# Values of block 2's attention made token-major, in eight weight units ahead of the head pairs

## The reference

```python
def dilated_attention_mixer(u, w_in, w_out, cos, sin):          # layer 0
    q, k, v = jnp.split(u @ w_in, 3, axis=-1)
    q = apply_partial_rope(split_heads(q, A_HEADS), cos, sin)   # 16 heads of 64
    k = apply_partial_rope(split_heads(k, A_HEADS), cos, sin)
    v = split_heads(v, A_HEADS)
    ...  # three banded softmaxes, combined by their denominators
    return merge_heads(o).astype(u.dtype) @ w_out

def differential_attention_mixer(u, w_in, w_out, ..., sub_g, cos, sin, layer_idx):  # layer 1
    q, k, v = jnp.split(u @ w_in, 3, axis=-1)
    ...  # 8 heads, each with two q/k halves of 64 and a value of 128
        sc = jnp.einsum('bhcqd,bhckd->bhcqk', qblk, k) * scale
        p = jax.nn.softmax(sc, axis=-1)
        a = p[:, :, 0] - lam * p[:, :, 1]
        return jnp.einsum('bhqk,bhkd->bhqd', a, v)
    o = rms_norm(o, sub_g) * (1.0 - lam_init)
    return merge_heads(o).astype(u.dtype) @ w_out
```

## Time and profile before

| | |
|---|---|
| median of three runs | 3102.79 us (3102.61, 3102.79, 3104.38) |
| span of the profiled execution | 3103.3 us |
| its time less its span | no separate time of it is shown; the span lies 0.5 us over the median and inside the three runs |
| TensorE busy | 3044.2 us, 98% |
| VectorE busy | 1775.0 us, 57% |
| ScalarE busy | 1269.9 us, 41% |
| GpSimd busy | 302.2 us, 10% |
| granted TensorE clock, mean | 0.996 |
| chain that ended last: TensorE | 83% of the span |
| the same chain: VectorE | 7% |

### The profile page before, as it was taken

The page is one execution under the profiler, slowest core; times in us unless marked ns, Lnnn a source line. Parts: engine busy times, 40 slices in busy tenths (PEclk is TensorE's granted clock), DMA queues, the critical chain, the costliest instruction groups (busy, mean ns, idle before and its releaser), DMA issues.

```text
span 3103.3 us, 38484 instructions
## 1 busy us (share of the span) xinstructions
PE 3044.2 (98%) x15248; PEld 2423.5 (78%) x15248; DVE 1775.0 (57%) x2564; ACT 1269.9 (41%) x2084; POOL 302.2 (10%) x257
## 2 busy tenths in 40 slices
PE   7999999999999999999999999999999999999998
PEld 6777888887777888887667878888866688788886
DVE  7765543457765544457775635344577755354444
ACT  6654422245654322344444534232344444342322
POOL 2011100011011100012001102000110011020001
PEclk9999999999999999999999999999999999999999
DMA  3111333232111223322112322332211123123332
GB/s 139 55 49 55 95 97 100 95 95 82 56 46 65 95 95 98 98 95 74 55 55 89 122 68 82 95 99 99 89 61 55 48 95 111 66 89 97 101 95 82
DMA packets 73726, 259.14 MB, mean 84 GB/s; under 512 B 8020, under 2 KB 10200, under 8 KB 73176
## 3 DMA queue, kind: packets, MB, share of 16 engines
q1 hardware_dynamic: 72824, 252.99, 25.8%
q0 software_dynamic: 736, 3.87, 0.4%
HBM read 254.73 MB, written 2.10 MB: 83 GB/s over the span
## 4 chain that ended last, share of the span: by engine, by line
PE 83%; DVE 7%; issue 6%; ACT 1%; DVEq 1%; POOLq 1%; DMA 1%; POOL 0%; ACTq 0%; SPq 0%
PE bank L563 68%; PE bank L493 2%; PE bank L1125 1%; DVE w_lo L2177 1%; PE bank L1136 1%; PE bank L779 1%; PE bank L1350 1%; PE bank L1329 1%; POOLq L3057 1%; PE bank L1080 1%; PE bank L1146 1%; PE bank L1150 1%; PE bank L809 0%; PE bank L822 0%; DMA w_raw<-weights 0%
## 5 line engine op out<-in xcount | busy, mean ns | idle before, releaser
L563 PE MATMUL bank<-a_hi,w_hi 128*128 128x512 f32 x2120 | 848.5, 400 | 18.8 <-DVE w_lo L2177 15.2
L563 PE MATMUL bank<-a_hi,w_lo 128*128 128x512 f32 x2120 | 828.4, 391 | 0.0
L563 PE MATMUL bank<-a_lo,w_hi 128*128 128x512 f32 x2120 | 827.5, 390 | 0.0
L2177 DVE TENSOR_TENSOR w_lo<-w_raw,w_hi 128x1024 fp32r<-128x1024 f32 (+1 forms) x474 | 609.4, 1287 | 285.7 <-ACT w_hi L1456 284.1
L1456 ACT ACTIVATE w_hi<-w_raw 128x1024 fp32r<-128x1024 f32 (+1 forms) x474 | 495.5, 1046 | 417.7 <-DMA w_raw<-weights 417.5
L563 PE MATMUL bank<-b_hi,w_hi 128*128 128x512 f32 (+1 forms) x1516 | 572.0, 377 | 2.6 <-DVE w_lo L2177 1.5
L563 PE MATMUL bank<-b_hi,w_lo 128*128 128x512 f32 (+1 forms) x1516 | 563.7, 372 | 0.0
L563 PE MATMUL bank<-b_lo,w_hi 128*128 128x512 f32 (+1 forms) x1516 | 563.5, 372 | 0.0
L563 PEld LDWEIGHTS bank<-a_hi,w_hi 128*128 128x128 f32 x2120 | 399.4, 188 | 120.1 <-issue 22.2
L563 PEld LDWEIGHTS bank<-a_hi,w_lo 128*128 128x128 f32 x2120 | 399.2, 188 | 85.7
L563 PEld LDWEIGHTS bank<-a_lo,w_hi 128*128 128x128 f32 x2120 | 399.8, 189 | 83.1 <-issue 3.8
(11 more groups left out here) (339 smaller groups left out, 3216.6 us busy)
## 6 DMA issues: line engine op xcount, KB each, us to landing
w_raw<-weights SPq DMA_DIRECT2D x458, 512.0 KB, 3.5
w_raw<-weights SPq DMA_DIRECT2D x16, 384.0 KB, 3.0
x<-x SPq DMA_DIRECT2D x8, 256.0 KB, 7.2
mem<-mem POOLq DMA_DIRECT2D x2, 1024.0 KB, 5.1
out<-x SPq DMA_DIRECT2D x8, 256.0 KB, 2.1
mem<-mem SPq DMA_DIRECT2D x1, 1024.0 KB, 11.7
ple<-ple POOLq DMA_DIRECT2D x2, 512.0 KB, 3.9
o<-c_level SPq DMA_DIRECT2D x1, 512.0 KB
```

The costliest lines, as they stand in the source:

```text
L563: last = mm(bank[unit_bank(u) if at is None else at][:, 0:cols], w[:, u % SLOTS, ks], t[:, k, 0:cols], start=(k == begun and n == 0), stop ...
L2177: tt(w_lo[:, u % SLOTS, w], w_raw[:, u % SLOTS, w], f32(w_hi[:, u % SLOTS, w]), ALU.subtract).then_inc(w_lo_ready, 1)
```

## The change

The stream of units gets another order: q and k of pair 0, then all values, then q and k of pairs 1 to 7. The values come in eight transfers that hold two contraction tiles of four units each. TensorE multiplies them the other way round (`values`): the activations of 128 tokens stand still and 512 value features stream, so that the result is token-major at once, in four banks for each half of the features. ScalarE copies each bank to `v` with the norm's root as its scale. Transposes, evictions and copies of the value units in the pairs are gone, and so is one unit in each pair. The half units stand in four places of a pair instead of six, and turn 3 of a pair moves ahead of the first score of the next. In layer 0 the last pair multiplies three output units at once, and five units follow; its output tiles stand one by one between the steps. All `kept_busy` of the two mixers go, but for five matmuls in layer 1. ScalarE's and VectorE's lists are rewritten to fit.

```diff
+order += [(at, 8, 0), (at + 8, 8, 0)]
+order += [(at + 16 + 4 * side, 0, rows) for side in range(2) for rows in range(4)]
+order += [(at + 8 * part + r, 8, 0) for r in range(1, 8) for part in range(2)]
...
+V_BANKS = (((3, 4, 6, 5), (2, 4, 6, 5)), ((3, 4, 6, 2), (5, 4, 6, 2)))
...
-        pe.wait_ge(bank_free, first if u == first + 2 else u - 1)
+        pe.wait_ge(bank_free, u - 1)
+        last.then_inc(unit_done, 1)
+        c.unit += 1
+def values(side, midway=None):
+    for j in range(4):
+        u = c.unit
+        pe.wait_ge(w_lo_ready, u + 1)
+        if side == 0 and j == 0:
+            pe.wait_ge(bank_free, first)
+        for tb in range(ST):
+            if side == 1 and j == 0:
+                pe.wait_ge(bank_free, first + 2 + tb)
+            out_ = bank[V_BANKS[l][side][tb]][:, :].rearrange("p (n c) -> p n c", n=4)
+            for i in range(2):
+                k = 2 * j + i
+                whole, rest = (t[:, u % SLOTS, :].rearrange("p (n c) -> p n c", n=4)[:, :, qs(i)] for t in (w_hi, w_lo))
+                for n, (x_, w_) in enumerate(((a[0], whole), (a[0], rest), (a[1], whole))):
+                    last = mm(out_, x_[:, k, qs(tb)], w_, start=(k == 0 and n == 0), stop=(k == 7 and n == 2))
+            if midway is not None and j == 0 and tb == 1:
+                midway()
         last.then_inc(unit_done, 1)
         c.unit += 1
...
         if p == 0:
-            pe.wait_ge(bank_free, first + 3)
+            pe.wait_ge(bank_free, first + 2 + V_UNITS)
...
-half(1)
-for r in range(1, PAIRS + 1):
-    more = r < PAIRS
-    if more:
-        half(0)
...
+    values(0, midway=columns_and_spread)
+values(1)
+half(0)
+for r in range(1, PAIRS):
+    half(1)
+    if r > 1:
+        turn(r - 2, 3)
     score(r - 1, 0)
-    if r >= 2:
+    half(0)
+    if r > 1:
         outputs(r - 2)
-    if more:
-        half(1)
     score(r - 1, 1)
     turn(r - 1, 0)
-    if more:
+    half(1)
+    score(r - 1, 2)
+    turn(r - 1, 1)
+    if r < PAIRS - 1:
         half(0)
     score(r - 1, 3)
     turn(r - 1, 2)
-    values(r - 1)
...
+    if diff and r > 1:
         tile_sums(r - 2)
+p = PAIRS - 1
+turn(p - 1, 3)
+score(p, 0)
+outputs(p - 1)
...
-    out_begun((4, 5))
-    outputs(PAIRS - 1)
-    kept_busy(F_S[0], 3, 2 * P)
-    out_begun((6, 7))
-a_units(6)
+    three = (0, 1, 2)
+    out_begun(0, three)
+    score(p, 1)
+    turn(p, 0)
+    out_begun(1, three)
+    score(p, 2)
+    turn(p, 1)
+    out_begun(2, three)
+    score(p, 3)
+    turn(p, 2)
+    out_begun(3, three)
+    turn(p, 3)
+    out_begun(4, three)
+    outputs(p)
+    out_begun(5, three)
+    out_begun(6, three)
+    out_begun(7, three)
+    a_units(5)
...
+def values(side):
+    act.wait_ge(unit_done, first + 6 + 4 * side)
+    for tb in (1, 2, 3, 0):
+        f(v[:, tb, 4 * P * side:4 * P * (side + 1)], bank[V_BANKS[l][side][tb]][:, :], ACT.Copy,
+          scale=root_cols[:, tb:tb + 1]).then_inc(bank_free, 1)
...
+ahead(first + 8)
+act.wait_ge(bank_free, first + 2)
+values(0)
+ahead(first + 12)
+values(1)
+for r in range(1, PAIRS):
+    if r > 1:
+        copies(r - 2, 3)
     exps(r - 1, 0)
+    ahead(first + 2 * r + 10)
     exps(r - 1, 1)
     copies(r - 1, 0)
+    if diff and r > 1:
         norm_square(r - 2)
     exps(r - 1, 2)
     copies(r - 1, 1)
+    ahead(first + 2 * r + 11)
     exps(r - 1, 3)
     copies(r - 1, 2)
...
+p = PAIRS - 1
+ahead(first + 26)
 if diff:
+    norm_root(0, 0, 24)
+copies(p - 1, 3)
+if not diff:
+    out_rounded((0,))
+exps(p, 0)
+if not diff:
+    out_rounded((1,))
+exps(p, 1)
+copies(p, 0)
+exps(p, 2)
+copies(p, 1)
+out_rounded((1,) if diff else (2, 3))
+exps(p, 3)
+copies(p, 2)
+out_rounded((2, 3) if diff else (4, 5))
+copies(p, 3)
...
+dve.wait_ge(bank_free, first + 2 + V_UNITS)
+for r in range(1, PAIRS):
+    if r > 1:
+        normalise(r - 2, 3)
     maxima(r - 1, 0)
+    evict(r, 0)
     normalise(r - 1, 0)
+    rope_sin(r, 0)
+    ahead(first + 2 * r + 10)
+    if r > 1:
         take(r - 2)
     maxima(r - 1, 1)
+    rope_add(r, 0)
     normalise(r - 1, 1)
+    if diff and r > 1:
         dve.drain()
         norm_clamped(r - 2)
+    evict(r, 1)
     maxima(r - 1, 2)
+    rope_sin(r, 1)
     normalise(r - 1, 2)
     maxima(r - 1, 3)
+    rope_add(r, 1)
+    ahead(first + 2 * r + 11)
+p = PAIRS - 1
+normalise(p - 1, 3)
+ahead(first + 26)
+maxima(p, 0)
...
+normalise(p, 0)
+take(p - 1)
...
+else:
+    out_low((1,))
+normalise(p, 1)
+maxima(p, 2)
...
+    out_low((1,))
+else:
+    out_low((2,))
+normalise(p, 2)
+maxima(p, 3)
...
```

More of the change, by code:

```diff
@@ L1152, in outputs, with out_begun @@
                     last.then_inc(f_out, 1)
[L1154 to L1170, removed]
+                def out_begun(k, begun=(0, 1)):
+                    u = c.unit
+                    if k == 0:
+                        pe.wait_ge(w_lo_ready, u + begun[-1] + 1)
+                        pe.wait_ge(bank_free, first + 3 * PAIRS)
+                        if 2 in begun:
+                            pe.wait_ge(f_sin, 2 * (pairs + PAIRS))
+                    pe.wait_ge(h_ready, c.since(h_ready, k + 1))
+                    for v_ in begun:
+                        last = products(u + v_, k, a, 8, S, at=(W_BANK + (OUT_THIRD,))[v_])
                         if k == 7:
                             last.then_inc(unit_done, 1)
[L1173 to L1176, removed]
+                    if k == 7:
+                        c.unit += len(begun)
+                        c.add(h_ready, 8)
                 def norm_sums(tiles):
                     pe.wait_ge(n_squared, tiles[-1] + 1)
+                    pe.wait_ge(n_applied, 6)
                     for i, p in enumerate(tiles):
@@ L1226, in fused @@
                         half(0)
-                    else:
-                        kept_busy(W_BANK[0] if diff else F_R, 3, 2 * P)
-                    score(r - 1, 2)
-                    if not more and diff:
-                        norm_spread(0)
-                        norm_spread(1)
-                    turn(r - 1, 1)
-                    if more:
-                        half(1)
-                    else:
-                        kept_busy(F_R, 3, 2 * P)
-                    score(r - 1, 3)
@@ L2737, in out2, with kept @@
                 for k in range(8 if mixed else 6):
-                    step(lambda u, b: dve.tensor_copy(y[:, k, :], b[:, :]).then_inc(bank_free, 1))
+                    def kept(u, b):
+                        b = bank[OUT_THIRD] if mixed and l == 0 and k == 2 else b
+                        dve.tensor_copy(y[:, k, :], b[:, :]).then_inc(bank_free, 1)
+                    step(kept)
                     if mixed and k == 2:
@@ L2842, in fused @@
                 rope_sin(0, 0)
-                evict(0, 2)
+                ahead(first + 4)
                 rope_add(0, 0)
                 rope_sin(0, 1)
-                ahead(first + 4)
+                ahead(first + 5)
                 rope_add(0, 1)
-                for r in range(1, PAIRS + 1):
-                    more = r < PAIRS
-                    if more:
-                        ahead(first + 3 * r + 2)
-                    if l == 0 and r == 1:
-                        dve.wait_ge(dil_landed, c.count(dil_landed, 16))
+                c.unit += V_UNITS
```

211 lines of the change are left out of this document (92 added, 119 removed).

## The result

The changed kernel takes 3140.07 us (median of four runs, 3138.57 to 3141.63), the kernel before 3103.43 beside it. The ratio is 1.0116 with a 95% interval of 1.0104 to 1.0129. That is 36.6 us slower; forecast were 17.4, with an upper end of 3130. The same kernel timed once more gave 3141.18 (ratio 1.0123, 1.0107 to 1.0138). All eight runs of the changed kernel, in two sessions, lie between 3137.41 and 3143.52. The profiled execution took 3138.57 us with a span of 3136.7, 33.4 over the span before; executions differ by some us, and what follows accounts for these 33.4.

A forecast was written before the change was run, and what follows sets the result against it. TensorE was taken to bound the kernel, with VectorE's long chain behind each score. Layer 0 +2.1, layer 1 +11.3 and clock +4 gave 17.4 us over the median of 3102.79: 3120.2 us, range 3103 to 3130.

The forecast's parts named there:

- Heads: Mixer start to pair 0's first score: 63.5 us in layer 0 against 23.95 before, 70.3 in layer 1 against 31.54.
- the wait of 1.9 behind the value copies: In each head, q1's first half waits for up to three of ScalarE's last four value copies: 1.9 us, bounds 0 and 2.5.
- the bare root in layer 1: Layer 1's head: ScalarE's root and VectorE's reciprocal lie uncovered between column sums and spread, 0.7 us, bounds 0.5 and 1.5.
- Pairs: Seven pairs of each mixer: 158.7 us in layer 0 against 195.9 before, 161.4 in layer 1 against 191.58.
- turns 2 and 3: Layer 1's pairs: TensorE waits for VectorE's chain, about 0.8 us at turn 2 and 0.4 at turn 3.
- the small wait of 0.15 us: Layer 0's pairs: TensorE waits 0.15 us a pair for VectorE's normalisation behind `w_lo`, giving 23.1 us a pair.
- Ends: Last pair's scores, outputs and tiles: 38.7 us in layer 0, 46.0 in layer 1 against 43.25 before.
- The walk: Both ends, followed wait by wait through the engines' chains: 38.7 us in layer 0, 46.0 in layer 1.
- two falls: Of six long empty waits, two lower TensorE's clock, some 2 us each: 4 us, bounds 0 and six falls.
- Rival (b): The clock falls at each of the six long waits: 12 us on top of 3116, so 3128 us; chance 0.18.
- other engines use half of the low stretch: Argument against a fall at all six long waits: these hang on other engines, which use half of the low-clock time.
- one output unit fewer: Behind layer 0's mixer: one unit of 5.44 us less follows, so the end counts 33.3 us instead of 38.7.

The follow-up runs named there:

- d1: The changed kernel with VectorE's key eviction put behind the third maxima and its second weight remainder behind the last normalisation, in every pair of both layers: 3129.90 us.
- f1: The changed kernel with useless filler matmuls put back into TensorE's waits in pair 6 and the last pair of both layers: 3128.03 us.
- bf_b: The kernel before with all useless filler matmuls of the two mixers taken out: 3113.06 us against 3104.16.
- after_b: The changed kernel itself timed and profiled once more, unedited, as a control: 3141.18 us.
- u2: The changed kernel with two output units in layer 0's last pair instead of three, and six units behind it instead of five: 3135.14 us.
- o2: The changed kernel with ScalarE's weight rounding put ahead of its squares and memory roundings behind layer 0's mixer, from the third step on: 3129.23 us.
- s1_b: The changed kernel with the third and fourth scores and norm spreads 2 and 3 ahead of output tiles 0 and 1 in layer 1's last pair: 3129.46 us.
- q1_b: The changed kernel with second query and key units released once the first pair's units are evicted, not when the value copies are done: 3132.39 us.
- after: The changed kernel itself, as first timed and profiled: 3140.07 us.
- l0_only: The change in layer 0 alone, with layer 1 as in the kernel before: 3117.86 us.
- r1_b: The changed kernel with ScalarE's rounding of tile 2 ahead of the third exponentials in layer 0's last pair: 3134.00 us.
- l1_only: The change in layer 1 alone, with layer 0 as in the kernel before: 3123.77 us.

## Why the prediction failed

Direction and the waits in heads, pairs and last pairs were right. The price of the low clock was not, one term was missing, and so the range ended too low.

- *Heads.* 63.5 and 70.3 us against 63.8 and 70.6 (the terms as written add up to 63.6 and 70.4). The value units at the price of the earlier trace rows, the wait of 1.9 behind the value copies (2.02), the bare root in layer 1: right. That layer 0's head came out so close has some luck in it: in seven of nine profiles the clock falls behind that wait and the head takes 65.3 to 65.4.
- *Pairs.* Layer 0: 20.8, 23.1, 22.5 against 20.97, 23.2, 22.6. Layer 1: 22.1, 23.2, 23.2 against 22.3, 23.3, 23.7. The waits stand at turns 2 and 3 as named. d1 bears out the small wait of 0.15 us that the forecast put into layer 0's pair for VectorE's `w_lo`: with `w_lo` (and the eviction) moved the period fell by 0.25. It is d1's own expectation, no wait there, that was wrong.
- *Ends.* 38.7 and 46.0 against 41.8 and 55.6, but 38.6 and 45.9 with the clock held up (f1). The long waits stand where they were named: 3.5 us before tile 2 in layer 0 (3.9 forecast), 3.7, 3.0 and 2.4 before tiles 0, 1 and 2 in layer 1 (4.0, 3.3 and 3.2). The walk was right.
- *Clock: the step that failed.* I added "two falls" of "some 2 us": 4. The fillers give back 12, in f1, and their loss costs 9 in the kernel before (bf_b). Rival (b) named six places and 12 us, and for the ends it is what happened: 3.1 and 9.6 us in this execution, in which the clock fell again and again in layer 1's end (no window of 10 us above .84) and slowed outputs, scores and tiles on the chain itself. Layer 1's part is a long draw; 5.0 was usual. I wrote against (b) that other engines use half of the low stretch. f1 shows little of that: these engines wait for just those matmuls, and tile to tile went from 8.8 to 6.7 us. And falls came behind waits of 2 us too (after_b), which I had not counted.
- *Behind layer 0's mixer: the term that was missing.* I priced "one output unit fewer" at -5.44. It is a unit of cover too. The VectorE and ScalarE loop behind the mixer shortens by 2.1 us only, so TensorE met two waits and another fall; 6.2 us up to the second spread. u2 and o2 remove it in two different ways.
- *Sum.* 17.4 less the 4 for the clock is 13.4. With 3.1 and 9.6 in the ends, 6.2 behind layer 0's mixer, 2.5 in heads and pairs, and 1.4 less in all the rest, it is 33.4, the difference of the spans.

What stays open: d1, o2 and s1_b gained 4 to 6 us more in time than the places that they touch usually show in the traces, q1_b 1.5. Some of that may be the draw of a single profile. From its start to its second spread layer 0 takes 306.1 to 308.7 us in the four profiles that leave it as changed (after, after_b, l0_only, s1_b), layer 1 323.9 to 328.6 in the six that leave it so (after, after_b, u2, o2, r1_b, l1_only). Falls of the clock that come in some executions and not in others would do that, and make such differences at the units and last pairs of the table above, but no run here shows that they account for the surplus.

## What to carry to other kernels

When an edit takes cover away, walk the chains as usual, and then walk them again with the matmuls behind each long wait at half rate (here falls came behind waits of 2.0 to 3.7 us, though not each time). The first walk gives the time with the clock held up, as f1 had it, and the second a cautious upper end in place of a surcharge of some us; no kernel here was forecast by it. A unit removed from TensorE's line is worth its length only if the loop of the other engines beside it is shorter than what is left. And before useless matmuls are dropped along with an old order, look at which waits of the new one need them.

## What the hardware showed unexpectedly

The same wait of 2.02 to 2.03 us, in the same kernel, at the same place, left the clock at full rate in one execution and at half rate for 3.6 us in another. Over all profiles with that wait the unit behind it was slow in 9 of 18 cases, by 1.6 us each time: seven of nine in layer 0, two of nine in layer 1. And separate edits that each shorten one wait gained up to twice what had been expected of them, but not so together: the medians of the single edits add up to 57 us, all of them at once gave 35 to 36.
